# A ring of four score slots, and the scaling of the exponentials on GpSimd, in a two-layer decoder trunk

## The reference, cut to what matters

```
p = jax.nn.softmax(jnp.where(cvis, s, NEG_INF), axis=-1) * cvis      # compressed keys: 31 (padded to 32)
o_c = jnp.einsum('bqhgc,bchd->bqhgd', p, vc)
...                                                                   # o_s (selected), o_w (window) likewise
return gates[..., 0:1] * o_c + gates[..., 1:2] * o_s + gates[..., 2:3] * o_w
```

## Time and profile before

| what | value |
|---|---|
| median of three timed executions | 3237.4 us (3234.8 to 3240.34) |
| the profiled execution, from its first to its last instruction | 3243.3 us |
| TensorE's mean granted clock in it | 0.878 |
| PE busy | 2740.9 us (85%) |
| DVE busy | 1546.4 us (48%) |
| ACT busy | 1158.8 us (36%) |
| POOL busy | 208.8 us (6%) |

### The profile page before, as it was taken

The page is one execution under the profiler, slowest core; times in us unless marked ns, Lnnn a source line. Parts: engine busy times, 40 slices in busy tenths (PEclk is TensorE's granted clock), DMA queues, the critical chain, the costliest instruction groups (busy, mean ns, idle before and its releaser), DMA issues.

```text
span 3243.3 us, 42636 instructions
## 1 busy us (share of the span) xinstructions
PE 2740.9 (85%) x13390; PEld 2155.2 (66%) x13390; DVE 1546.4 (48%) x3661; ACT 1158.8 (36%) x2392; POOL 208.8 (6%) x237
## 2 busy tenths in 40 slices
PE   1899889958989776999949998897689995699997
PEld 1676667747767554888828676675577774478885
DVE  2334665556355454443232566555663545444422
ACT  1323444435244343222221344353433433432222
POOL 5000000000000303000030000000000002200000
PEclk7866889979999867999968788898899997599998
DMA  6200001111311211333332110111112132023332
GB/s 124 73 27 20 27 27 53 56 33 40 84 53 40 91 52 36 94 97 97 93 77 68 33 27 27 39 53 56 33 53 78 40 96 67 14 78 97 97 94 69
DMA packets 327931, 195.48 MB, mean 60 GB/s; under 512 B 12541, under 2 KB 322929, under 8 KB 326865
## 3 DMA queue, kind: packets, MB, share of 16 engines
q1 hardware_dynamic: 324768, 177.23, 18.8%
q0 software_dynamic: 2992, 16.13, 2.1%
HBM read 186.00 MB, written 7.34 MB: 60 GB/s over the span
## 4 chain that ended last, share of the span: by engine, by line
PE 72%; DVE 10%; issue 7%; ACT 4%; POOL 4%; DMA 1%; DVEq 0%; ACTq 0%; POOLq 0%; SPq 0%
PE acc L960 53%; PE scores L960 6%; PE o_acc L960 5%; PE turn L1055 4%; POOL square_sum L644 2%; DVE work L1380 2%; PE acc L1170 2%; DVE work L1406 1%; ACT y_hi L801 1%; ACT w_hi L682 1%; DVE h_lo L1294 1%; PE scores L1001 1%; DMA head_sink<-in_swa_sinks_dram 1%; DVE q_lo L1369 1%; PE scores L1005 1%
## 5 line engine op out<-in xcount | busy, mean ns | idle before, releaser
L960 PE MATMUL acc<-h_hi,w_hi 128*128 128x512 f32 (+1 forms) x1888 | 792.9, 420 | 31.9 <-DVE h_lo L1294 28.5
L960 PE MATMUL acc<-h_hi,w_lo 128*128 128x512 f32 (+1 forms) x1888 | 769.5, 408 | 0.0
L960 PE MATMUL acc<-h_lo,w_hi 128*128 128x512 f32 (+1 forms) x1888 | 769.4, 407 | 0.0
L1271 DVE TENSOR_TENSOR w_lo<-w_f,w_hi 128x1024 fp32r<-128x1024 f32 x336 | 411.1, 1224 | 494.7 <-ACT w_hi L682 486.4
L960 PEld LDWEIGHTS acc<-h_hi,w_hi 128*128 128x128 f32 (+1 forms) x1888 | 368.7, 195 | 163.1 <-DVE h_lo L1294 58.8
L682 ACT ACTIVATE w_hi<-w_f 128x1024 fp32r<-128x1024 f32 x336 | 353.9, 1053 | 267.2 <-PE acc L960 264.4
L960 PEld LDWEIGHTS acc<-h_hi,w_lo 128*128 128x128 f32 (+1 forms) x1888 | 368.7, 195 | 85.0 <-issue 3.8
L960 PEld LDWEIGHTS acc<-h_lo,w_hi 128*128 128x128 f32 (+1 forms) x1888 | 369.9, 196 | 71.7 <-issue 3.8
L729 ACT ACTIVATE p_hi<-turn 128x256 fp32r<-128x256 f32 (+4 forms) x416 | 164.0, 394 | 428.7 <-PE turn L1055 428.5
L783 ACT ACTIVATE work<-work,neg_max 128x256 f32<-128x256 f32 (+4 forms) x416 | 210.1, 505 | 197.7 <-DVE neg_max L1380 196.4
L1055 PE MATMUL turn<-ident,work 128*128 128x128 f32 (+1 forms) x880 | 188.8, 304 | 94.1 <-DVE work L1406 91.8
(11 more groups left out here) (236 smaller groups left out, 3838.4 us busy)
## 6 DMA issues: line engine op xcount, KB each, us to landing
w_f<-in_ffn_w_in_dram SPq DMA_DIRECT2D x88, 512.0 KB, 3.7
w_f<-in_w_gate_dram SPq DMA_DIRECT2D x64, 512.0 KB, 3.9
w_f<-in_w_in_dram SPq DMA_DIRECT2D x62, 512.0 KB, 3.9
w_f<-in_w_branch_dram SPq DMA_DIRECT2D x32, 512.0 KB, 3.4
w_f<-in_ffn_w_out_dram SPq DMA_DIRECT2D x32, 512.0 KB, 3.9
w_f<-in_w_out_dram SPq DMA_DIRECT2D x16, 512.0 KB, 4.0
w_f<-in_ffn_w_out_dram SPq DMA_DIRECT2D x16, 384.0 KB, 3.4
x_spill<-trunk POOLq DMA_DIRECT2D x2, 2048.0 KB, 8.1
```

Of the source, the lines that this page charges most:

```text
L960: ins = nc.tensor.matmul(dst, a, b, start=(n == 0 and not added), stop=(n == count - 1))
L1271: nc.vector.tensor_tensor(w_lo[:, u % 2, :], w_f32[:, u % 2, :], w_hi[:, u % 2, :].bitcast(F32), ALU.subtract).then_inc(w_ready, 1)
```

## The change

`work` and `squares` become one tile `ring` of four slots of 512 columns. The passes use slot s % 4 for step s, so bias_scores(s) now waits for turn_probs(s-4). Outside the passes the old names stay, as the first and the second half of the ring. VectorE keeps the inversion of the sum. The multiplication with the gate (L1402) and the scaling (L1406) leave VectorE, and GpSimd does both with one instruction that has two scalars per partition: the inverse sum and the gate (in the ungated passes only the inverse sum). GpSimd waits for `inverted`, TensorE for `divided` as before, now raised by GpSimd. The calls stand in GpSimd's stream in the order of the passes.

```
+RING = 4
...
-        squares = sb("squares", [P, 2, S])
-        work = sb("work", [P, 2, S])
+        ring = sb("ring", [P, RING, S])
+        work, squares = ring[:, 0:2, :], ring[:, 2:4, :]
...
+            def divide(l, ps):
+
+                st = l * (4 * NHD) + 4 * HB[ps.name]
+                for s in range(ps.steps):
+                    h, i = divmod(s, NT)
+                    c = slice(s % 4, s % 4 + 1)
+                    p = ring[:, s % RING, 0:ps.keys(i)[1]]
+                    wait_apart(pool, inverted, st + (s + 1))
+                    if ps.gate is None:
+                        nc.gpsimd.tensor_scalar(p, p, over_sum[:, c], None, ALU.mult).then_inc(divided, 1)
+                    else:
+                        nc.gpsimd.tensor_scalar(p, p, over_sum[:, c], coef[:, ps.gate, i, h:h + 1], ALU.mult,
+                                                ALU.mult).then_inc(divided, 1)
...
                 power(l, "mix_pre")
+                wait_apart(pool, ng_coef, l * 2 + 2)
+                for ps in (CMP, SEL, WIN, SWA):
+                    divide(l, ps)
                 power(l, "mlaq")
                 power(l, "mlakv")
+                divide(l, MLA)
+                divide(l, FOX)
                 wait_apart(pool, split_ready, l * NSP + SPB["merged"] + KT)
                 pool.dma_start(trunk[:, :, :], x_spill).then_inc(x_back, 16)
...
                 pool.dma_start(m_f32, mem_hat).then_inc(mem_back, 16)
+                divide(l, XA)
...
-                    nc.scalar.activation(work[:, s % 2, 0:w], work[:, s % 2, 0:w], ACT.Exp,
+                    nc.scalar.activation(ring[:, s % RING, 0:w], ring[:, s % RING, 0:w], ACT.Exp,
...
-                        ins = nc.tensor.transpose(bank[0:w, t * P:(t + 1) * P], work[:, s % 2, t * w:(t + 1) * w],
+                        ins = nc.tensor.transpose(bank[0:w, t * P:(t + 1) * P], ring[:, s % RING, t * w:(t + 1) * w],
...
-                    dve.wait_ge(turned, l * NTN + (TB[ps.name] + s + 1))
+                    dve.wait_ge(turned, l * NTN + (TB[ps.name] + max(s - RING + CREDIT, 0) + 1))
...
-                        work[:, s % 2, 0:w], scores[s % 2][:, 0:w], bias(ps, i), ps.slope(h),
+                        ring[:, s % RING, 0:w], scores[s % 2][:, 0:w], bias(ps, i), ps.slope(h),
...
                     nc.vector.reciprocal(over_sum[:, c], total).then_inc(inverted, 1)
-                    by = over_sum[:, c]
-                    if ps is CMP and s == 0:
-                        dve.wait_ge(ng_coef, l * 2 + 2)
-                    dve.wait_ge(inverted, st + (s + 1))
-                    if ps.gate is not None:
-                        by = whole_sum[:, c]
-                        nc.vector.tensor_tensor(by, over_sum[:, c], coef[:, ps.gate, i, h:h + 1],
-                                                ALU.mult).then_inc(gated, 1)
-                        dve.wait_ge(gated, st + (s + 1))
-                    w = ps.keys(i)[1]
-                    nc.vector.tensor_scalar(work[:, s % 2, 0:w], work[:, s % 2, 0:w], by, None,
-                                            ALU.mult).then_inc(divided, 1)
```

More of the change, by code:

```diff
@@ L356, in build @@
         inverted = sem("inverted")
-        gated = sem("gated")
         divided = sem("divided")
@@ L1598, in _ @@
                 attend(l, WIN, PJ_K["win"])
-                dve.sem_inc(gated, 4 * (NHD - HB["swa"]))
                 branch(l, 0)
```

## The result

The changed kernel took 3308.5 us (median of four runs, 3271.0 to 3333.1). The kernel before, run beside it, took 3236.1 us (four runs, 3211.1 to 3240.3). The ratio is 1.022, with an interval of 1.016 to 1.029: slower by 2.2%. The prediction was 3228 us in a range of 3190 to 3272, so it is wrong, in sign and beyond its range.

The account below looks back on a forecast made before the run. The prediction took TensorE, busy 85% of the span, as the bound, its scaling waits of 91.8 us being the most to win. Terms -15 - 0.5 + 13.5 + 1 - 12 + 4 = -9 gave 3228 us, range 3190 to 3272.

Parts of the forecast that it names:

- One operation comes to GpSimd, on every chain: Scaling moved to GpSimd: 0.60 us at 384 columns, 0.49 at 256, 0.31 at 32; +13.5 us over 71 ungated waits.
- sort (2): Ungated waits where y_lo or stagings precede the scaling in VectorE's order: the ring gains nothing, GpSimd's scaling costs +13.5 us.
- sort (1): Waits in SEL and WIN where VectorE's bias waits for a transpose to free its slot: the ring removes them, -15 us.
- A first scaling like that is +1: GpSimd's first scaling would be slow, as its first select was at 1.23 us against 0.21: +1 us.
- CMP, -0.5: Shorter scaling waits in CMP, 0.36 us instead of 0.46, and in nsa_rest: half a microsecond gained in all.
- the clock of CMP, -12: In CMP one of two clock falls would come one staging later or not at all: 8 steps, -12 us.
- MLA's clock, +4: Longer waits at MLA's outs would bring two or three clock falls of 1.7 us each: +4 us.
- Shared access to SBUF: 0: VectorE's two-input w_lo contending with GpSimd's scaling would stand on no chain: 0, at worst +5 us.
- Rival A: GpSimd scales at its sums' rate, 0.97 us at 384 columns, on the chain behind y_lo: 3266 us, chance 0.22.
- B: CMP's clock stays up in both layers, -45 us for -12: 3195 us, chance 0.13.
- C: CMP's clock falls just as before: 3240 us, chance 0.18.
- D: No slot wait goes, because VectorE's low part waits for the transpose as the slot did: 3252 us, chance 0.07.

Follow-up runs that it names:

- The ring alone: The kernel before the change with only the ring of four slots added, gate and scaling staying on VectorE: 3202.9 us, ratio 0.994.
- the old order: VectorE inverts step s-1 behind the bias of round s; the changed kernel with the inverse one round earlier took 3167.4 us, ratio 0.982.
- Two scalars: The changed kernel with a column of ones as second scalar and multiplication in GpSimd's ungated scaling: 3245.8 us, ratio 1.005.
- the best version: The changed kernel with VectorE's inverse one round earlier and constant 1.0 as second operation in GpSimd's ungated scaling: 3156.5 us, ratio 0.979.

## Why the prediction was wrong

- **The step that failed** is "One operation comes to GpSimd, on every chain", in its price. The prediction took 0.60 us for the scaling at 384 columns and 0.49 at 256, from the select. The ungated ones took 1.24 and 0.93 in MLA's rounds, beyond even the upper bound of 0.97 and 0.65 from GpSimd's sum. The gated ones took 0.67, 0.56 and, at 32 columns, 0.37, close to the 0.60, 0.49 and 0.31 taken. So the estimate was right for the form with two operations and wrong by a factor of two for the form with one, which is the one on the long waits. Its own sign of being wrong, a scaling of over 0.8 us, came. An estimate "by the nearest row" was made once for two different forms.
- The hand-over from VectorE was right (0.17 for 0.15). The one to TensorE was 0.15 for 0.05, 7 us over 72 waits; the rows of before had it at 0.15 behind VectorE's scaling, and 0.05 counted a gain of 0.10 that no row of this chain gave. With the hand-overs as measured and the form with two scalars, the term would have been about +0.37 a wait; the experiment gave +0.43.
- The term of sort (2): +13.5 us taken, bounds +6 to +33; measured 134.4 - 72.5 = +61.9, 0.86 a wait. The places and the number of waits were right: 72 for 71, and the timeline shows the chain that was described. Some 6 us of the 61.9 are the collision with `w_lo` in SWA.
- The term of sort (1): -15 us taken; the gated waits fell by 8.2. What is left in SEL and WIN is 2.4 to 2.6 us a pass, not the 1 us a layer that was forecast. The passes shortened by 12.7 us all the same, some of it clock. The ring alone, with the scaling on VectorE, took 7.7 of 16.7 us of waits away in SEL and WIN. Its 0.5% or 18 us look like the 15 forecast, but by luck of the clock: the mechanism did half of it.
- "A first scaling like that is +1": it isn't there. No gated scaling of 32 columns took more than 0.37 us.
- "CMP, -0.5" and "the clock of CMP, -12": neither came. From inverse to transposes it takes 0.84 us, not 0.67, and the wait grew to 0.54. CMP took 81.5 and 81.2 us after 81.5 and 69.3. But in the old order waits of 0.46 to 0.54 us go with passes of 57 to 82 us, so the difference isn't shown to be the change's.
- "MLA's clock, +4": right in kind, too small. The longer waits brought falls in MLA, SWA and FOX of both layers, some 27 us beyond the waits. Two scalars, with 28 us less of waits in these passes, has about 23 us of it back.
- "Shared access to SBUF: 0" was wrong by some 6 us: `w_lo` was said to stand on no chain, and in SWA it ran into six scalings on which TensorE waited. The other shapes met none (128 columns: 604 to 612 ns) until the order changed.
- Rival A had the right place, the right sign and the right turning point: it said that a scaling of 0.61 us at 384 columns decides, and the form with two scalars, at 0.67, came out 0.5% slower. Its time of 3266 was 42 us short: its price was too low by 0.28 us, and it gave the clock 11 us. The chance of 0.22 was too small; "hardly above what I take" should have been read as a coin toss. B and C were about CMP's clock and weren't decided. D, that no slot wait goes, is refuted, though only half of them went. The chances also hold a slip: A, D, the rest and a fifth of C add up to 0.38 for "slower than 3244", not 0.35.

The sum with measured terms: -8 for the slots, +62 for the chain, together 53.7 of waits, +32 of clock, 86 of the 88 us between the two profiled runs. Against the -9 forecast that is 95 us: 48 from the price of the chain, 7 from the slots, and 40 from the clock (+32 for -8), of which 25 are CMP's (-12 forecast, +13 measured).

Open: why CMP's clock falls at one staging and not at the next with the same wait (without the wait it never fell there); and whether the remaining 37.8 us of waits for the low part in the best version can be had by moving only that of the rounds with an out. That wasn't tried.

## What to carry to other kernels

Before an operation goes to another engine, ask whether it stands on the chain from one use of the bottleneck to the next; if it does, the other engine's duration and one more hand-over (here 0.17 us) are paid each time, and the relief of the first engine brought nothing that could be measured here. First move it off that chain in the engine's own order, and only then to another engine: the same offload cost 35 to 90 us in one order and gained 14 to 27 in another. Look at what the first engine starts right behind the hand-over, too: its next instruction may hold up the other engine. And take no duration of an instruction from a neighbour with another number of operands or operations without a bound that is wide enough to say so.

## What the runs showed of the hardware

- GpSimd's `tensor_scalar` with one multiplication takes 606, 1245 and 1567 ns at 128, 384 and 512 columns. With a second multiplication by a column it takes 452, 666 and 773; by an immediate 371, 585 and 693.
- GpSimd's scaling of 128 columns went from 0.61 us to 1.47 when VectorE's `w_lo` of 1.23 us, with two inputs in SBUF, started 0.22 us ahead of it, and one of 256 columns from 0.93 to 1.99 when `w_lo` started 0.07 us after it. `w_lo` kept its 1.22 to 1.23 us both times.
- From the end of VectorE's inverse to the start of GpSimd's scaling it takes 0.17 us, from the end of a scaling to TensorE's transposes 0.15, on GpSimd as on VectorE.
- A wait of TensorE of 0.46 to 0.54 us in CMP was sometimes followed by a granted clock of 0.50 to the end of the pass and sometimes not; a pass takes 57.2 us without it and 81.5 with it. Without that wait (12 passes) the clock didn't fall there. Two passes with the fall take 49 us more than two without; the kernel before spreads over 44 us in all its runs.
